# Reordering the startup loads of a two-block transformer kernel, and moving two modulation chunks into the first attention

## The reference, cut to what matters

```python
def hybrid_layer(x, ctx, c, c_ctx, ...):
    shift, scale, gate = jnp.split(jax.nn.silu(c) @ w_mod + b_mod, 3, axis=-1)     # 1024 x 3072 weights
    shift_c, scale_c, gate_c = jnp.split(jax.nn.silu(c_ctx) @ w_mod + b_mod, 3, axis=-1)
    h = rms_norm(x, norm_w) * (1.0 + scale[:, None, :]) + shift[:, None, :]
    hc = rms_norm(ctx, norm_w) * (1.0 + scale_c) + shift_c
    p = h @ w_in                                   # 2592 columns: MLA, GQA, convolution, output gates
    ...                                            # two attentions and a depthwise convolution
    y = jnp.concatenate([o_mla, o_gqa, o_conv], axis=-1) * jax.nn.silu(p[..., OFF_GATE:])
    x_new = x + gate[:, None, :] * (y @ w_out)     # gate is first used here
```

## Time and profile before

| what | value |
|---|---|
| three runs | 2508.99, 2509.06, 2500.67 us |
| span of the profiled execution (first to last instruction) | 2501.5 us; no other time of this execution is given |
| mean granted TensorE clock, share of the full one | 0.944 |
| busy: TensorE, VectorE, ScalarE, GpSimd | 2279.8, 1285.8, 1135.0, 1045.9 us |
| SP issues x, ctx | at 0.70, 1.22 us |
| ACT issues the table | at 0.70 us |
| attention of layer 0, of layer 1, differential | about 267 to 413, 633 to 725, 955 to 1027 us |

### The profile page before, as it was taken

One profiled execution on the slowest core, in us unless ns is written; L12 is line 12 of the kernel. 1 busy time (PEld: TensorE's weight loads), 2 busy tenths in 40 slices (PEclk: granted clock), 3 DMA queues, 4 the chain that ended last, 5 costly groups with the idle time before them and its releaser, 6 DMA issues.

```text
span 2501.5 us, 29397 instructions
## 1 busy us (share of the span) xinstructions
PE 2279.8 (91%) x11181; PEld 1716.6 (69%) x11181; DVE 1285.8 (51%) x1616; ACT 1135.0 (45%) x1242; POOL 1045.9 (42%) x477
## 2 busy tenths in 40 slices
PE   6899787989887999889998799999999999999997
PEld 4454344567356644689998687787878787878786
DVE  1102674112642025355542376867777777777775
ACT  2211332122323004344432376767667676767674
POOL 1001930002600000000000197988979797979794
PEclk8899888989886999989999799999999999999998
DMA  9311343122661215225562499998989898989890
GB/s 322 112 50 67 135 173 112 59 83 101 239 219 68 101 68 196 74 102 202 157 192 90 168 349 331 336 360 309 374 295 375 293 375 294 375 295 373 297 369 18
DMA packets 258284, 532.12 MB, mean 213 GB/s; under 512 B 5850, under 2 KB 41201, under 8 KB 258076
## 3 DMA queue, kind: packets, MB, share of 16 engines
q1 hardware_dynamic: 255808, 527.06, 59.1%
q10 hardware_dynamic: 1948, 3.80, 0.4%
q0 software_dynamic: 448, 0.15, 0.0%
HBM read 529.93 MB, written 1.05 MB: 212 GB/s over the span
## 4 chain that ended last, share of the span: by engine, by line
PE 51%; POOL 29%; issue 10%; DVE 6%; ACT 2%; DMA 1%; ACTq 0%; POOLq 0%; DVEq 0%
PE bank L659 48%; POOL ring_r L645 17%; POOL scratch_r L645 12%; PE bank L697 1%; DVE nmax L1692 1%; DVE scratch L1782 1%; PE bank L756 1%; ACT H L1287 1%; PE bank L726 1%; DVE scratch L1760 1%; ACT L1254 1%; DVE scratch L1788 0%; DMA ring<-in_w_mod 0%; ACTq L1232 0%; DVE H L1633 0%
## 5 line engine op out<-in xcount | busy, mean ns | idle before, releaser
L645 POOL TENSOR_TENSOR ring_r<-ring,H_r 128x384 fp32r<-128x384 f32 x128 | 339.3, 2659 | 868.5 <-ACT H_r L1525 867.9
L659 PE MATMUL bank<-H_r,scratch_r 128*128 128x512 f32 (+1 forms) x2016 | 542.6, 346 | 22.1 <-DVE scratch_r L2055 11.9
L659 PE MATMUL bank<-H,ring 128*128 128x256 f32 (+2 forms) x1408 | 454.9, 486 | 25.5 <-ACT H L1287 22.5
L659 PE MATMUL bank<-scratch_r 128*128 128x512 f32 (+1 forms) x1696 | 419.7, 361 | 1.8 <-issue 1.8
L659 PEld LDWEIGHTS bank<-H,ring 128*128 128x128 f32 (+1 forms) x1408 | 271.9, 194 | 203.9 <-issue 158.0
L659 PEld LDWEIGHTS bank<-H_r,scratch_r 128*128 128x128 f32 x2016 | 351.3, 191 | 67.6 <-issue 15.0
L659 PEld LDWEIGHTS bank<-scratch_r 128*128 128x128 f32 x1696 | 304.1, 189 | 50.9 <-issue 2.0
L1525 ACT ACTIVATE H_r<-ring 128x2048 fp32r<-128x2048 f32 x128 | 244.8, 1918 | 99.3 <-PE bank L659 99.2
L1237 ACT ACTIVATE scratch<-bank 128x512 f32<-128x512 f32 (+6 forms) x166 | 84.6, 509 | 451.3 <-PE bank L659 341.6
L2038 DVE TENSOR_TENSOR ring_r<-ring,H_r 128x1664 fp32r<-128x1664 f32 x128 | 254.7, 2000 | 57.6 <-ACT H_r L1525 56.3
L659 PE MATMUL bank<-H_r,modrow_r 128*128 128x512 f32 x672 | 263.0, 391 | 0.0
(11 more groups left out here) (193 smaller groups left out, 3028.2 us busy)
## 6 DMA issues: line engine op xcount, KB each, us to landing
ring<-in_moe_w SPq DMA_DIRECT2D x96, 2048.0 KB, 8.1
scratch<-in_moe_w SPq DMA_DIRECT2D x72, 2048.0 KB, 8.4
ring<-in_ada_w SPq DMA_DIRECT2D x24, 2048.0 KB, 8.0
ring<-in_ff_w SPq DMA_DIRECT2D x14, 2048.0 KB, 7.7
ring<-in_w_mod SPq DMA_DIRECT2D x12, 2048.0 KB, 8.1
ring<-in_ff_w SPq DMA_DIRECT2D x8, 1792.0 KB, 8.4
ring<-in_w_in SPq DMA_DIRECT2D x6, 2048.0 KB, 7.8
ring<-in_attn_w_qkv SPq DMA_DIRECT2D x6, 2048.0 KB, 7.9
```

Source lines behind the costliest of these rows:

```text
L645: nc.gpsimd.tensor_tensor(low_half(h)[:, own], raw_half(h)[:, own], HI_PARTS[h % HI_RING][:, own].bitcast(F32), ALU.subtract).then_inc(lo_ ...
L659: m = nc.tensor.matmul(out_, w, x_, start=first, stop=last)
```

## The change

It does four things. SP no longer waits for the small vectors before the first weight load. The table is laid out anew and loaded in two parts: what the start needs (identity, selection, reduction columns, 80 KB) first, the rest (1488 KB) after ACT's small vectors. The router and the four columns of `lqk` leave `small_loads`, so that twelve loads each are left to ACT and to POOL; the five are loaded last, on ACT's queue, with a semaphore of their own, and what uses them waits for that. And the two gate chunks of `mod0` are no longer loaded and used before layer 0. They stand in the list behind layer 0's `small` chunk and are the first two pairs of its attention's fill, which then has 14 pairs; `attention_steps` spaces the pairs evenly over the units, where before it placed them at a whole-number gap. That moves the pairs of the other fills too: those of the differential attention from units 0, 2, 4, 6, 8, 10 to 0, 3, 6, 8, 11, 14.

```diff
-T_ID, T_ONES, T_ROT, T_ROT32 = 0, 128, 256, 384
-T_COS, T_SIN, T_COS32, T_SIN32 = 416, 672, 928, 1184
-T_DFT, T_DFTC, T_DFTS, T_IOTA, T_UPPER, T_SEL, T_PART, T_RED, T_ALL = 1440, 1696, 2208, 2720, 2976, 3104, 3106, 3107, 3136
+T_ID, T_SEL, T_PART, T_RED, T_FRONT = 0, 128, 130, 131, 160
+T_ONES, T_ROT, T_ROT32 = 160, 288, 416
+T_COS, T_SIN, T_COS32, T_SIN32 = 448, 704, 960, 1216
+T_DFT, T_DFTC, T_DFTS, T_IOTA, T_UPPER, T_ALL = 1472, 1728, 2240, 2752, 3008, 3136
...
-    return (mods(0) + inner0 + mods(1) + mods2[:MODS2_FIRST] + out0 + inner1 + mods2[MODS2_FIRST:]
+    return (mods(0)[:4] + inner0 + mods(0)[4:] + mods(1) + mods2[:MODS2_FIRST] + out0 + inner1 + mods2[MODS2_FIRST:]
...
-        FILL = [[(1, c) for c in range(6)] + [(2, c) for c in range(MODS2_FIRST)],
+        FILL = [[(0, 4), (0, 5)] + [(1, c) for c in range(6)] + [(2, c) for c in range(MODS2_FIRST)],
...
-            gap, sent = units // len(fill), 0
+            sent = 0
...
-                if u % gap == 0 and sent < len(fill):
+                if sent < len(fill) and sent * units <= u * len(fill):
...
-        small_loads.append((router[:, :, :], a["moe_router_2"][0].rearrange("(k p) e -> p k e", p=P)))
-        small_loads += [(lqk[:, i:i + 1], a[name].rearrange("a d -> d a"))
+        late_loads = [(router[:, :, :], a["moe_router_2"][0].rearrange("(k p) e -> p k e", p=P))]
+        late_loads += [(lqk[:, i:i + 1], a[name].rearrange("a d -> d a"))
...
-            sp.wait_ge(vectors_landed, VECTORS_IN)
             for i, (_, parts) in enumerate(chunks):
...
+                pe.wait_ge(table_rest_landed, 16)
                 group([(rot32, KR[64:96, 0:LAT])], lambda bk: bk[64:96, 0:LAT])
...
-            for c in range(6):
+            for c in range(4):
                 mod_pair("mod first", (0, c))
                 if c:
                     mod_pair("mod second", (0, c - 1))
-            mod_pair("mod second", (0, 5))
+            mod_pair("mod second", (0, 3))
...
+            pe.wait_ge(late_landed, LATE_IN)
             pe.wait_ge(lam_in, 1)
...
-            act.dma_start(tab[:, :], table).then_inc(table_landed, 16)
+            act.dma_start(tab[:, 0:T_FRONT], table[:, 0:T_FRONT]).then_inc(table_landed, 16)
             for dst, src in small_loads[::2]:
                 act.dma_start(dst, src).then_inc(vectors_landed, 16)
+            act.dma_start(tab[:, T_FRONT:T_ALL], table[:, T_FRONT:T_ALL]).then_inc(table_rest_landed, 16)
+            for dst, src in late_loads:
+                act.dma_start(dst, src).then_inc(late_landed, 16)
...
                 turns = []
+                written(*mod_last[m])
                 for k in range(KT):
...
+                if l == 0:
+                    dve.wait_ge(late_landed, LATE_IN)
+                    v.tensor_tensor(lprod[:, :], lqk[:, 0:4:2], lqk[:, 1:4:2], ALU.mult).then_inc(lam_in, 1)
+                    dve.wait_ge(table_rest_landed, 16)
                 b, n = ready()
                 rotate(KR[64:96, 0:LAT], bank[b][64:96, 0:LAT], cos32, sin32, ROTS[64:96, 0:LAT], b)\
...
             dve.wait_ge(vectors2_landed, VECTORS2_IN)
-            v.tensor_tensor(lprod[:, :], lqk[:, 0:4:2], lqk[:, 1:4:2], ALU.mult).then_inc(lam_in, 1)
```

More of the change, by code:

```diff
@@ L338, in build @@
         table_landed = sem("table_landed")
+        table_rest_landed = sem("table_rest_landed")
+        late_landed = sem("late_landed")
         vectors_landed = sem("vectors_landed")
@@ L560, in build @@
         small_loads.append((dwrows[0:2 * CONV_K, :], a["conv_dw_w"].rearrange("l k c -> (l k) c")))
-        small_loads.append((router[:, :, :], a["moe_router_2"][0].rearrange("(k p) e -> p k e", p=P)))
-        small_loads += [(lqk[:, i:i + 1], a[name].rearrange("a d -> d a"))
+        late_loads = [(router[:, :, :], a["moe_router_2"][0].rearrange("(k p) e -> p k e", p=P))]
+        late_loads += [(lqk[:, i:i + 1], a[name].rearrange("a d -> d a"))
                         for i, name in enumerate(("attn_lq1_2", "attn_lk1_2", "attn_lq2_2", "attn_lk2_2"))]
         VECTORS_IN, VECTORS2_IN = 16 * len(small_loads[::2]), 16 * len(small_loads[1::2])
+        LATE_IN = 16 * len(late_loads)
         @block.sync
@@ L1411, in _ @@
                     mod_step("mod second", (0, c - 1))
-            mod_step("mod second", (0, 5))
+            mod_step("mod second", (0, 3))
             for l in range(2):
```

## The result

The changed kernel takes 2512.94 us (median of 12 runs, 2510.6 to 2516.5), the kernel before 2505.14 us (12 runs on the same chip, 2500.24 to 2511.21). The ratio is 1.0029, with a 95% interval of 1.0017 to 1.0040. The profiled execution has a span of 2509.1 us, where before it was 2501.5. In the runs where both are known, a run's time is its span plus 1.9 us; so 1.9 of the 7.5 us between span and median in the table ahead of the prediction are this offset, and 5.6 were scatter of the runs.

A forecast was written before the change was run, and what follows sets the result against it. The startup was taken to wait for the vectors' last piece, layer 0's attention to have TensorE and VectorE taking turns. -14.0 - 2.3 + 7.2 + 0 = -9.1 us gave 2500 us against 2508.99; range 2488 to 2511.

The forecast's parts named there:

- The start: Stretch up to H: four chunks instead of six gain 14.0 us, and the vectors' earlier landing gains 2.3.
- term of 14.0: Before layer 0: four modulation chunks instead of six let H start at about 50.2 instead of 64.43, taken as 14.0 us.
- term of 2.3 for the loads: Small vectors at the start: first transpose at 13.8, a gain of 2.7, of which 2.3 us was taken.
- rival in which the small loads are caught behind the weights: At the start: vectors land at 34 instead of 16.49, +17.5 us, time 2520; chance 0.10.
- the chunks moved out bring nothing: Before layer 0: `in.q` or H late anyway, gain of 14.0 falls towards 2, sum +3 us; chance 0.03.
- ScalarE's hold-up: At the start: ScalarE, issuing late loads, is free at 18.5; first square ready at 20.8, needed at 21.3.
- Moved pairs: Layer 0's and the third attention's pairs moved to other units cost 0 us, bounds -2 to +4.
- Two more pairs: Layer 0's attention: each second pair in a two-unit group costs 3.6 us, 7.2 for both, bounds 2.1 and 10.4.
- rival of cheap pairs: Layer 0's attention: extra pairs cost 1.07 us each, sum -14.2 us, time 2495; chance 0.23.
- No wait for `ring<-in_w_mod`: Sign before layer 0: TensorE no longer waits for the modulation weights' load.
- H's first scaling: Sign before layer 0: H's first scaling near 48 us, where before it was 64.43.
- Attention of layer 0 grows by over 10: Sign against the prediction: layer 0's attention was to take 153 us instead of 146; growth over 10 us refutes it.

The follow-up runs named there:

- Kernel 3: The kernel before with the new loads alone; six chunks still ahead of layer 0, pairs at their old places: 2502.52 us, ratio 1.0003.
- Kernel 5: The kernel before with layer 0's twelve pairs at units 1, 3, ..., 23 instead of 0, 2, ..., 22: 2535.57 us, ratio 1.0126.
- 6: The kernel before with the differential attention's six pairs at units 0, 3, 6, 8, 11, 14: 2507.92 us, ratio 1.0018.
- kernel 2: The changed kernel with the differential attention's pairs put back and layer 0's 14 pairs at all even units plus 1 and 3: 2498.48 us, ratio 0.9982.
- kernel 9: The changed kernel with the pair before the values in odd units, same work, loads and units: 2489.78 us, ratio 0.9923.
- 10: New loads, gate chunks beside H and the `in` products, old pair places, odd units' pair before the values: 2487.03 us, ratio 0.9917.
- 1: The changed kernel with only the differential attention's pairs put back at units 0, 2, 4, 6, 8, 10: 2505.73 us, ratio 1.0019.
- 7: The kernel before, old loads, with the gate chunks in layer 0's attention at the changed kernel's places: 2505.42 us, ratio 1.0005.
- 4: The changed loads, gate chunks beside H and between the `in` products, attention pairs at the places of before: 2495.15 us, ratio 0.9970.

## Why the prediction was wrong

**The start: right, with the wrong shares.** The forecast was -16.3 to H; it is -18.4 to the spread and -19.3 to `in.q`. Kernel 3 and the changed one differ at the start in the two chunks alone, and have like column sums (8.84 and 9.14 us); their spreads are 13.7 apart, so the term of 14.0 holds. The spread took 1.14 us, as assumed. The term of 2.3 for the loads is mis-sized: the first transpose moved by 0.6, because POOL's last load took 8.8 us from its issue instead of 6.4:

```profile
scratch<-in_conv_dw_w POOLq DMA_DIRECT2D x1, 62.0 KB, 8.8
```

I had said that more traffic behind it would change this little. The Trainium skill's page "DMA: Bandwidth & Descriptors", section "Issuing engines are not separate DMA queues", says that loads from all issuing engines interleave on the same 16 engines. The trace agrees with that for this load; it got 2.4 us dearer beside the weights. The rival in which the small loads are caught behind the weights fell: 15.89, not 34. So did the one in which the chunks moved out bring nothing. The rest of the start's gain, 4.7 us, is 0.6 for the first transpose and otherwise mostly luck: column sums of some 9 or some 11 us occur with old and new loads (last section). So the forecast of the start came out near the measured value partly because this luck stood where the loads' term failed. The first transpose (13 to 15 forecast) came at 15.89.

**ScalarE's hold-up: harmless as forecast, earlier than forecast.** Table load at 14.22, not 17 to 20; the first square at 19.30, needed at 22.45. I had let the held issue go 2.3 us after the rest of the table had landed. It was released at 6.77 + 4.92 = 11.69, while the rest of the table, issued at 5.83, landed only at 16.2:

```profile
tab<-in_table ACTq DMA_DIRECT2D x1, 1488.0 KB, 10.4
```

**"Moved pairs": the step that failed.** The prediction said "No row shows a single pair in an odd unit" and "the work of the number of pairs stays, so I take 0 and keep -2 to +4". Kernels 5 and 6 measure it: 3.1 us for a pair moved to an odd unit in layer 0, 3.05 in the differential attention. The changed kernel has six odd pairs in layer 0 (7, 9, 11, 19, 21, 23) and eight even ones. At 3.1 for an odd pair and nothing for an even one that is 18.6, where its stretch grew by 15.0; kernel 2, with two odd pairs, would be at 6.2 and is at 2.2 to 3.6, one of the two standing at unit 1, where there are no values yet. Counting a pair by TensorE's work was the error. An even unit's values are transposes alone, so a pair behind them runs while the other engines are at work. In an odd unit the product of values first waits for VectorE; when it ends, the other two have little or nothing left to do until the next scores, which stand behind the pair. The code shows that (`if qt == 1`), so it could have been read before any run; I looked for a row and, finding none, took 0 out of bounds of -2 to +4; the moved places measured 12.1 + 6.2 = 18.3 us. The range shows the same gap: its lower end takes this step's -2, its upper end leaves out the +4. With it the sum at that end would be +2.4 instead of -1.6, and the time 2515 instead of 2511.

**"Two more pairs": the mechanism right, the size off.** 2.2 to 3.6 us in kernel 2 instead of 7.2, at the low end of my bounds of 2.1 to 10.4. The groups of the earlier trace rows hold a second pair in an odd unit, so their 3.6 us held part of the price of that place. How much is not fixed: kernels 9 and 10 have 136.5 and 136.2 us in layer 1, against 140.7 to 146.4 in the ten others, and the order changes five of its pairs (unit 1 has no values). With all 14 pairs in harmless places (kernel 9) layer 0's stretch is 2.6 above before. The rival of cheap pairs, 1.07 us each, was nearer to it here than my 3.6, and still gave a gain, since it too priced the places at 0.

**The tests that the prediction named.** No wait for `ring<-in_w_mod`: right. H's first scaling (near 48) and `in.q` (near 55.5): earlier, 45.13 and 52.61. Attention of layer 0 grows by over 10: it was named as what would make it wrong, and it did (15.0).

**The sum again, with what was measured:** -19.4 (start and H) + 2.9 (two more pairs) + 12.1 (places in layer 0) + 6.2 (places in the differential attention) + 3.1 (layer 1, chance) + 2.7 (the rest) = +7.6. The forecast had -16.3 + 7.2 + 0. So the stretches that the edit touches give +1.8, and 5.8 us lie where it changed nothing. Against these stands the start's luck: without the 5.8 and without some 4.1 us of luck in the -19.4 (an estimate from the 4.7 and 0.6 above), the sum is +5.9, near the 7 us that the ratio says.

What stays open: how much of the price of an odd pair would be left at the full clock. No run here holds the clock and the order apart. The changed kernel's trace says that some is left. Of its six odd pairs in layer 0 three ran at the lower clock and three, those at units 11, 19 and 23, at the full one. At unit 19 the pair ends at 376.11, and the other two engines had still been waiting:

```profile
374.19 1.92 PE L662 MATMUL bank<-ring,cond 128*32 128x512 f32 x16
...
376.18 0.60 ACT L1245 ACTIVATE modrow<-bank 128x512 f32<-128x512 f32 x1 [4.69 <-PE bank L662]
...
377.20 1.29 DVE L1701 TENSOR_REDUCE nmax<-bank 128x1 f32<-128x512 f32 x2 [1.82 <-PE bank L662]
```

The 2.7 us of the rest lie in stretches in which nothing was changed (0.3 in the feed-forward, 1.6 in the Fourier layer, 1.5 in the experts, -0.7 in layer 1's products), and were not followed.

## What to carry to other kernels

Work that is put into the gaps of another loop has a price by its place, not by its length: ask of each place who is idle when it runs and what stands behind it on the same engine. In this kernel a filler belonged ahead of a wait, and not between the end of a wait and the instruction that feeds the other engines. When an edit spaces fillers evenly, look at which side of such a wait each one lands on; a change of units alone cost 37 us here, and turning two steps in the order gave back more than the whole startup edit brought.

## What the runs showed of the hardware

The granted clock of TensorE was often down behind such waits: behind the one of 3.22 us the eight matmuls of L729 took 1.87 us instead of 0.95 to 1.05, at a granted clock of 0.50, the lower of the two levels (1.2 against 2.4 GHz). The six odd pairs of layer 0 in the changed kernel stood behind waits of 3.46, 4.94 and 3.22 us (lower level) and of 2.52, 1.39 and 2.52 us (full). The Trainium skill's page "TensorE: Matmul & The Clock Gate", section "Loop structure matters more than you think", says that the loop nest decides whether matmuls stay at the full clock. Kernel 5 agrees (0.81 against 0.89); but only half of its loss is longer busy time.

The column sums at the start, the same 64 matmuls in all kernels, took 8.84 to 9.44 us in seven profiles (the changed kernel, 1, 2, 3, 5, 7, 9) and 11.12 to 11.39 in five (before twice, 4, 6 and 10), and nothing between. Both occur with the old loads and with the new. The granted clock goes with them: in all twelve profiles it is 1.00 up to 26 us, falls to 0.50 between 26 and 28, and is back at 1.00 between 33 and 37.5 us where the sums were short, and only from about 40 where they were long. The long sums also start later (23.59 to 23.97 against 21.66 to 22.64), as the transposes ahead of them took 7.6 to 7.9 us instead of 6.4 to 7.0 at a clock of 1.00. Why the transposes come in two lengths was not shown. The runs of kernel 3 fall in two groups about 6 us apart (around 2500.5 and 2506.7); whether that is the same thing was not shown.
